# The last output tile of a feed-forward stage multiplied in two halves of 128 tokens

## What is computed

```python
def swiglu(x, wi, wo):
    a, b = jnp.split(x @ wi, 2, axis=-1)
    return (jax.nn.silu(a) * b) @ wo

# in second_block, for the one layer:
    h = h + 0.5 * rmsnorm(swiglu(rmsnorm(h, n[4]), ffn2_wi[l], ffn2_wo[l]), n[5])
return h[:, N_META:]
```

## Time and profile before

| | |
|---|---|
| Time, median of 3 runs | 1010.59 us (1009.25 to 1010.59) |
| Time of the profiled execution | 1010.97 us |
| Its span in the trace | 1009.1 us |
| PE busy | 989.7 us, 98% of the span |
| PEld busy | 973.7 us, 96% |
| POOL busy | 752.5 us, 75% |
| DVE busy | 549.5 us, 54% |
| ACT busy | 486.5 us, 48% |
| Granted TensorE clock, mean over the span | 0.99 |

### The profile page before, as it was taken

How to read it: one execution, slowest core, us unless ns; L and a number is a source line. 1 busy time by engine, 2 the same in 40 slices (tenths; PEclk the granted TensorE clock), 3 DMA queues, 4 the chain that set the end, 5 groups by cost and what they waited for, 6 DMA issues and landing times.

```text
span 1009.1 us, 21532 instructions
## 1 busy us (share of the span) xinstructions
PE 989.7 (98%) x8151; PEld 973.7 (96%) x8151; DVE 549.5 (54%) x931; ACT 486.5 (48%) x749; POOL 752.5 (75%) x588
## 2 busy tenths in 40 slices
PE   9999999999999999999999999999999999999996
PEld 7999999999999999999999899999999989999996
DVE  5945984547644444601874783476656574445103
ACT  6634324446654444444566643433264564444541
POOL 2896666666999888999389844667549539999993
PEclk9999999999999999999999998999999999999998
DMA  9564434343565555565454223443226736665661
GB/s 308 178 200 142 125 106 134 120 143 97 177 194 182 177 169 174 159 176 183 135 172 147 88 85 101 126 136 116 86 82 189 236 101 198 194 190 181 185 179 56
DMA packets 48345, 154.63 MB, mean 153 GB/s; under 512 B 6060, under 2 KB 11188, under 8 KB 48280
## 3 DMA queue, kind: packets, MB, share of 16 engines
q1 hardware_dynamic: 46128, 151.33, 48.6%
q10 hardware_dynamic: 2152, 2.38, 0.7%
HBM read 151.59 MB, written 2.10 MB: 152 GB/s over the span
## 4 chain that ended last, share of the span: by engine, by line
PE 87%; DVE 6%; ACT 3%; POOL 2%; DMA 1%; issue 1%; SPq 0%; DVEq 0%; ACTq 0%
PE panel L1721 70%; PE panel L1779 3%; PE aux L1880 3%; POOL wlo L644 1%; DMA memk<-in_mem_panels 1%; PE aux L2134 1%; PE aux L2145 1%; PE panel L1815 1%; PE aux L2107 1%; DVE h L1107 1%; DVE tmp L1101 1%; PE aux L2175 1%; PE aux L2184 1%; PE aux L1787 1%; DVE xl L1090 1%
## 5 line engine op out<-in xcount | busy, mean ns | idle before, releaser
L644 POOL TENSOR_TENSOR wlo<-raw,whi 128x512 fp32r<-128x512 f32 x548 | 727.7, 1357 | 234.7 <-ACT whi L739 211.6
L1721 PE MATMUL panel<-xh,whi 128*128 128x256 f32 (+2 forms) x1440 | 416.9, 290 | 3.5 <-DVE xl L1090 1.3
L1721 PE MATMUL panel<-xh,wlo 128*128 128x256 f32 (+2 forms) x1440 | 409.9, 285 | 0.0
L1721 PE MATMUL panel<-xl,whi 128*128 128x256 f32 (+2 forms) x1440 | 409.5, 284 | 0.0
L739 ACT ACTIVATE whi<-raw 128x1024 fp32r<-128x1024 f32 x280 | 293.9, 1053 | 200.6 <-PE panel L1721 167.4
L1721 PEld LDWEIGHTS panel<-xh,whi 128*128 128x128 f32 x1440 | 273.3, 190 | 5.6 <-issue 2.0
L1721 PEld LDWEIGHTS panel<-xh,wlo 128*128 128x128 f32 x1440 | 273.3, 190 | 0.0
L1721 PEld LDWEIGHTS panel<-xl,whi 128*128 128x128 f32 x1440 | 272.8, 189 | 0.1
L1721 PE MATMUL panel<-hh,wlo 128*128 128x272 f32 (+1 forms) x352 | 100.5, 286 | 0.0
L1721 PE MATMUL panel<-hh,whi 128*128 128x272 f32 (+1 forms) x352 | 100.2, 285 | 0.0
L1721 PE MATMUL panel<-hl,whi 128*128 128x272 f32 (+1 forms) x352 | 99.9, 284 | 0.0
(11 more groups left out here) (336 smaller groups left out, 1575.2 us busy)
## 6 DMA issues: line engine op xcount, KB each, us to landing
raw<-in_panels SPq DMA_DIRECT2D x232, 512.0 KB, 3.5
raw<-in_down SPq DMA_DIRECT2D x32, 448.0 KB, 3.3
raw<-in_down SPq DMA_DIRECT2D x16, 512.0 KB, 3.5
memk<-in_mem_panels SPq DMA_DIRECT2D x4, 512.0 KB, 7.9
memx<-in_mem SPq DMA_DIRECT2D x4, 256.0 KB, 5.5
h<-in_x SPq DMA_DIRECT2D x1, 1024.0 KB, 8.6
spill<-h ACTq DMA_DIRECT2D x1, 1024.0 KB, 4.6
h<-spill ACTq DMA_DIRECT2D x1, 1024.0 KB, 7.2
```

The costliest lines, as they stand in the source:

```text
L644: ins = nc.gpsimd.tensor_tensor(wlo[:, slot, half], raw[:, slot, half], whi[:, slot, half].bitcast(f32), ALU.subtract)
L1721: ins = M(bank[:, 0:w], wt[:, slot, P * t:P * t + P], x[:, kk, c0:c0 + w], start=first and m == 0 and n == 0, stop=last and m == len(pairs ...
```

## The change

- `down_loop(1, ...)` and `norm_stat(8)` on TensorE are replaced by `down_in_halves()`. It walks over the 24 panels without a hardware loop, with the wait for `lo_ready` of every panel. Tiles 0 to 6 are multiplied as before. For tile 7 it multiplies all 22 slices for tokens 0 to 127 into one bank, and then for tokens 128 to 255 into the bank after it (that of tile 4). Each is 66 matmuls of 128 columns.
- The norm sum is made for each half. That of half 0 is put between the products of half 1, before slice 7; that of half 1 follows at the end.
- ACT squares, and takes logarithm and exponential, half by half. DVE copies half by half (with a wait of the copy on itself), and then for each half weighs 2 x (4 tiles x 128 tokens) and adds 2 x (4 tiles x 128 tokens).
- The four stores are now 4 tiles x 128 tokens each.

The diff without the renamed parameters of the helpers and the new semaphores:

```diff
-QUARTERS = [(0, 1), (2, 3), (4, 5), (6, 7)]
+QUARTERS = [(half, part) for half in range(2) for part in range(2)]
...
-    uses += [("stat", n) for n in (6, 7, 8)]
+    uses += [("stat", n) for n in (6, 7, 8, 9)]
...
+        def last_bank(half):
+
+            return pb[(DOWN2_O + 7 + half) % 4]
...
-            for t, u in QUARTERS:
-
-                sp.wait_ge(h_ready, tile_done(8, u))
-                sp.dma_start(a["out"][:, t:u + 1, :], h[:, t:u + 1, META:LEN]).then_inc(stored, 16)
+            for m, (half, part) in enumerate(QUARTERS):
+
+                t, r = slice(4 * part, 4 * part + 4), slice(P * half, P * half + P)
+                sp.wait_ge(h_ready, 8 + WEIGHED[8] + m + 1)
+                sp.dma_start(a["out"][:, t, r], h[:, t, META + P * half:META + P * half + P]).then_inc(stored, 16)
             sp.wait_ge(stored, 16 * len(QUARTERS))
...
-            square_out(DOWN2_O, DOWN2_P, 3, 8)
-            post_root(8)
+            square_out(DOWN2_O, DOWN2_P, 3, 8, KT - 1)
+            ahead(PANELS - 1)
+            for half in range(2):
+                r = slice(P * half, P * half + P)
+                act.wait_ge(last_half, half + 1)
+                A(sq[:, KT - 1, r], last_bank(half)[:, 0:P], ACT.Square).then_inc(last_squared, 1)
+                bank, use = aux("stat", 8 + half)
+                aux_wait(act, use)
+                order(A(lnt[:, r], bank[:, 0:P], ACT.Ln, scale=1.0 / 1024.0, bias=eps))
+                A(rstd[:, r], lnt[:, r], ACT.Exp, scale=-0.5).then_inc(rstd_ready, 1)
...
-            take_out(DOWN2_O, 8, 40, 0.5)
-            combine(8)
+            take_out(DOWN2_O, 8, 40, 0.5, tiles=KT - 1)
+            for half in range(2):
+                r = slice(P * half, P * half + P)
+                dve.wait_ge(last_squared, half + 1)
+                order(TS(tmp[:, KT - 1, r], last_bank(half)[:, 0:P], vcol("gains", 47), 0.5, ALU.mult, ALU.mult))
+                dve.wait_ge(rstd_ready, 9 + half)
+                for part in range(2):
+                    t = slice(4 * part, 4 * part + 4)
+                    TT(tmp[:, t, r], tmp[:, t, r], bc(rstd[:, r], 1, 4), ALU.mult).then_inc(weighed, 1)
+                for part in range(2):
+                    t, own = slice(4 * part, 4 * part + 4), slice(META + P * half, META + P * half + P)
+                    dve.wait_ge(weighed, WEIGHED[8] + 2 * half + part + 1)
+                    TT(h[:, t, own], tmp[:, t, r], h[:, t, own], ALU.add).then_inc(h_ready, 1)
...
+            def down_in_halves():
+
+                parts = [(0, 8), (8, 7), (15, 7)]
+                pe.wait_ge(hid_low, 2 * FT - 2)
+                for n in range(24):
+                    i, part = n // 3, n % 3
+                    o, (k0, size) = DOWN2_O + i, parts[part]
+                    pe.wait_ge(lo_ready, DOWN2_P + n + 1)
+                    if n == 2:
+                        pe.wait_ge(hid_low, 2 * FT)
+                    if i == KT - 1:
+                        continue
+                    if part == 0:
+                        pe.wait_ge(bank_free[o % 4], o // 4)
+                    products(pb[o % 4], n % RING, [(t, k0 + t) for t in range(size)], hh, hl, 0, ROWS,
+                             part == 0, part == 2).then_inc(passed, 1)
+
+                def last_stat(half):
+
+                    stat, use = aux("stat", 8 + half)
+                    aux_open(use)
+                    r = slice(P * half, P * half + P)
+                    if half == 0:
+                        pe.wait_ge(summed, 6)
+                    M(stat[:, 0:P], ones[:], sq[:, 0, r], start=True, stop=False)
+                    pe.wait_ge(last_squared, half + 1)
+                    M(stat[:, 0:P], ones[:], sq[:, KT - 1, r], start=False, stop=True).then_inc(aux_full, 1)
+
+                for half in range(2):
+                    o = DOWN2_O + KT - 1 + half
+                    pe.wait_ge(bank_free[o % 4], o // 4)
+                    for part, (k0, size) in enumerate(parts):
+                        ins = products(last_bank(half), (21 + part) % RING, [(t, k0 + t) for t in range(size)], hh, hl, P * half, P,
+                                       part == 0, part == 2, lambda kk: last_stat(0) if half and kk == 7 else None)
+                    ins.then_inc(last_half, 1)
+                last_stat(1)
...
-            down_loop(1, DOWN2_O, DOWN2_P, ROWS)
-            norm_stat(8)
+            down_in_halves()
```

More of the change, by code:

```diff
@@ L509, in build @@
         mg_low = sem("mg_low")
+        last_half = sem("last_half")
+        last_squared = sem("last_squared")
         raw_ready = [sem(f"raw_ready{i}") for i in range(RING)]
@@ L561, in build @@
         LATE = {4: 0, 6: 1, 8: 2}
-        TILES = {4: PAIRS, 6: PAIRS, 8: QUARTERS}
+        TILES = {4: PAIRS, 6: PAIRS}
         WEIGHED = {4: 0, 6: len(PAIRS), 8: 2 * len(PAIRS)}
@@ L791, in combined, with square_out @@
                 return lambda kk: act.wait_ge(h_ready, tile_done(n, kk))
-            def square_out(first_o, first_p, each, n):
-                for i in range(KT):
+            def square_out(first_o, first_p, each, n, tiles=KT):
+                for i in range(tiles):
                     ahead(first_p + each * i + each - 1)
@@ L1150, in low_panel, with take_out @@
                 TT(wlo[:, p % RING, :], raw[:, p % RING, :], whi[:, p % RING, :].bitcast(f32), ALU.subtract).then_inc(lo_ready, 1)
-            def take_out(first_o, n, at0, factor, low_behind={}):
+            def take_out(first_o, n, at0, factor, low_behind={}, tiles=KT):
                 w = W[n]
-                for i in range(KT):
+                for i in range(tiles):
                     o = first_o + i
```

## The result

The changed kernel takes 1025.55 us, the median of 20 executions (1011.64 to 1032.92), against 1009.48 for the kernel before (20 executions, 1004.73 to 1011.1).

A forecast was written before the change was run, and what follows sets the result against it. TensorE, busy 98% of the span, was taken as the bound, with 10.2 us exposed behind its last product. 1.9 + 7.0 + 0.4 - 2.7 = +6.6 at full clock; with half clock +19.2 on 1010.6, so 1030 us, range 1016 to 1034.

The forecast's parts named there:

- The sum at full clock: Whole change if TensorE's clock held: added stall, products and norm sum less the tail's saving, +6.6 us.
- the fall: TensorE clock halves about 1 us after the halves start, without recovery; products at 0.21 us, +19.2 in all; chance 0.62.
- The stall: TensorE idle before the halves, waiting for GpSimd's last low part (panel 24): 1.9 us added.
- Products: Last tile's 132 products of 128 columns, paced by weight loads at 0.112 us each: 14.8 against 7.8, 7.0 more.
- The inserted norm sum: First half's norm sum between the second half's products on TensorE: 0.4 us more at full clock, its other work hidden.
- The tail: Stretch from last product to end, 10.2 us before: 2.7 saved, 2.4 of it from four VectorE pieces instead of eight.
- The stores: Four final stores with 512-byte runs and twice the packets: 0.2 us longer, between 0 and 0.75.
- The loop written out: TensorE's body, a loop of two turns before, written out: nothing taken for it.
- the third rival: Streaming, not the weight load, paces the narrow products at 0.06 us: -0.3, 1010.3 us, not slower; chance 0.05.
- the mixer's falls: Two clock falls after TensorE idles earlier in the program, near 577 and 601 to 611, used as evidence; one short fall 1.7 us.
- the first (the clock holds: +6.6, 1016 to 1020): TensorE's clock holds or falls only briefly during the halves: +6.6, 1017.2 us, or 1019 with a short fall; chance 0.24.
- The second (two records to a product): Narrow products go like plain fp32, two records of 0.11 us each: +21.4 in all, 1032 us; chance 0.06.

The follow-up runs named there:

- experiment 5: Changed kernel with GpSimd making the last weight panel's low part twice, so TensorE idles longer before the halves: 1033.85, 1034.06, 1034.4 and 1034.5 us, ratio 1.0239.
- experiment 7: Changed kernel without the stall, the last tile's narrow products loading 64 weight columns instead of 128 (upper 64 features left out): 1005.96 us, ratio 0.9965.
- experiment 6: Changed kernel with the last tile kept as 66 wide products and the old order of waits, only the close going by halves: 1008.96 us, ratio 0.9978.
- experiments 5 to 8: Second group of four kernels: longer stall, close alone by halves, half the weight columns, halves streaming all 256 columns; the kernel before beside them had median 1010.59 or 1010.54.
- first group of runs: Four kernels: stall removed (1015.34 us), stall filled with matmuls (1013.65), stall alone before wide products (1009.48), stall and narrow products with the old close (1018.05).
- experiments 3 and 8: The second of this pair: changed kernel, stall kept, each half's 66 products streaming all 256 columns: 1016.08 us, ratio 1.0065.
- experiment 3: Kernel before with its loop written out and the last tile waiting for panel 24 at once, products and close unchanged: 1009.48 us, ratio 1.0007.

## Why the prediction was right and wrong

The median, 1025.55, lies in the range and 4.5 us under the forecast. The sum at full clock was right to 0.1 us, and the fall, forecast at 12.6 us, costs some 13.8. **What failed is the step that took the fall as certain**: "So I expect the fall, about 1 us after the start, and no recovery". "No recovery" held where the long fall came, in the trace of experiment 5 and, by times and mean clocks, in the upper group. That it would come did not hold: 12 of 20 executions have the long fall and 8 don't, and the forecast had one outcome at 0.62 and the other at 0.24 as if the kernel would be the one or the other. It is both, by execution. The mean of all 20 is 1022.7, 13.8 us above the kernel before and not 19; 6.6 and the fall's 13.9 in 12 of 20 executions would give 14.9.

Step by step, forecast and measured:

- **The stall**: 1.9; 1.93 measured, with the releaser that was named.
- **Products**: 0.112 each, 14.8 for all; 0.111 to 0.112, and 9.90 + 4.99 = 14.9. The reason held too (experiment 7). The Trainium skill, "TensorE: Matmul & The Clock Gate", section "Back-to-back issue gap", has about 81 ns at 128 columns; the trace doesn't agree, and the estimate of +2.5 us from it would have been 4 us short.
- **The inserted norm sum**: 0.4; 0.27 + 0.22 = 0.5. The rest of the first half's close was hidden, as forecast: its last addition ended at 1005.2, 1.5 us ahead of the last product's end, and its stores were issued at 1004.62 and 1005.22.
- **The tail**: 2.7 saved, to 7.5; the last product ends at 1006.66 and the span at 1014.0, 7.35, where it was 10.2, so 2.9 saved. VectorE 2.4 as worked out. The norm sum's matmul pair takes 0.50 where the one piece of the earlier trace rows took 0.71, 0.2 as forecast.
- **The stores**: 0.2 assumed, between 0 and 0.75. From the last addition to the end it is 3.0 in both kernels, so 0 on the path.
- **The loop written out**: nothing; experiment 6 has it too and is no slower than the kernel before.
- **The sum**: 6.6; 24.6 - 18.05 = 6.6.
- **The clock**: a full fall was priced at 19.2 - 6.6 = 12.6 us. Between the medians of the two groups lie 12.3, between their means 13.8, between the traces of experiment 5 and of the changed kernel 13.9. A product at half clock was taken at 0.21; it takes 0.213. In experiment 5 products and inserted norm sum take 28.95 us (995.62 to 1024.57) where the forecast had 27.6: the fall comes 0.3 us after the start, not 1.0, which puts 6 more products at 0.213 (0.6 us), 0.213 instead of 0.21 is 0.4 over the rest, and the inserted norm sum takes 0.96 where 0.8 was taken.
- **The chances**: the third rival, the one case not slower, has 0.05, but "same" and "faster" together only 0.04; the two don't agree by 0.01.

The 4.5 us between forecast and median are then these. The median falls into the lower end of the twelve, because eight executions lie below it; the twelve's own median is 1027.1, 1.6 higher. The forecast was added to 1010.6 for the kernel before, from three runs; over 20 it is 1009.5, 1.1 less. The other 1.8 I put on the mixer's falls, which the clocks show less often in these twelve: eight are at 0.980 or higher, which is some 41 us at half clock or less and leaves no room for the mixer's fall of 10 us beside the long one of 36; only four, at 0.976 or lower, have it. Of the 29 executions of the kernel before beside experiments 5 to 8 nineteen are at 0.992 or lower, 16 us and more at half clock; some 5.4 of these are the idle end of its span (1003.7 to 1009.1 is at 0.50), the rest needs the fall of 10. Why they should be rarer no run tells, and 20 executions may be luck. The means depend less on where a middle falls: the twelve lie 19.3 above the kernel before, where 19.2 was forecast. That is so close partly by luck, since the fall costs 1.2 more than its price and rarer falls in the mixer take about as much off.

The spread within each group is those falls, by the list of clocks. A span of 1009.8 at 0.999 has 2 x 0.001 x 1009.8 = 2 us at half clock, no more than the idle end of the profiled span, and one of 1015.5 at 0.992 has 16. In the upper group 1023.3 us (the execution of 1025.16) at 0.982 gives 37 us, just the length of experiment 5's fall (995.94 to 1032.1 is 36.2), and 1029.4 to 1030.2 us at 0.976 give 49, which is that and the two falls of the mixer, 3.4 and 10.2 (experiment 5's profile has all three, and 0.976). So all 20 times need only one kind of event at the end, present or not, on top of the spread that the kernel before has too. This is worked out from mean clocks, and wouldn't show a fall of 3.4 us behind the stall for certain; of an upper execution of the changed kernel there is no trace.

What the experiments settle of the fall, in executions that stand in an upper group:

```
idle before    products after      fell and stayed
none           narrow              0 of 11 (no stall)   0 of 8 (stall filled)
1.7 to 1.9     256 columns wide    0 of 12 (one wide tile)  0 of 12 (two wide halves)
1.7 to 1.9     narrow              12 of 20 (changed)   2 of 7 (old close)
4.85           narrow              4 of 4
```

In these runs both are needed, as the forecast had it. The idle sets it off, and the narrow stream keeps it down: behind wide products the clock fell for 3.4 us in both profiles and recovered. Within the first group of runs alone, for the idle ahead of narrow products, it is 2 of 7 against 0 of 19, which is thin; the case rests on the changed kernel's 12 of 20 and experiment 5's four beside it. What decides in which executions 1.9 us of idle are enough is open. The Trainium skill, "TensorE: Matmul & The Clock Gate", section "Why this matters for your kernels", warns only of idle gaps longer than these, so by it the clock holds in every execution. The traces of experiments 3 and 8 don't agree: falls after 1.72 and 1.93 us.

Of the rivals, the first (the clock holds: +6.6, 1016 to 1020) is what 8 of 20 executions did, at +5.3 by the medians and +5.5 by the means; the profiles put the change itself at 6.6. The second (two records to a product) is out: one record each at 0.112. The third (the stream sets the pace) is out in the changed kernel, and experiment 7, where the load is halved, gives what it promised: -2.3 in the end stage, where the rival's -0.3 without the stall of 1.9 is -2.2.

Could a version beat the kernel before? Without the stall the split costs 4.5 us. The close alone by halves gives 0.4 us in the trace, and 12 executions can't tell it from nothing. Splitting only the last of the three panels, which would add a third of the extra products, wasn't tried.

## What to carry to other kernels

Before you split a matmul's moving side to let the work behind it start earlier, look at what sets the spacing: if it is the weight load (here 0.111 us a product when 128 columns stream, 0.119 when 256 do), each half costs nearly as much as the whole, and the price is nearly the whole tile again (7.1 us for a tile of 7.8). When you write a loop of waits out by hand, see which wait comes to stand ahead of which work; here a wait that had belonged to the last third of a tile moved ahead of all of it. And count a short idle stretch by what follows it: ahead of wide products it cost up to 1.8 us more than itself here, ahead of a narrow stream it could halve the clock to the end, in some executions only, so that a few runs or one profile can miss it.

## What the runs showed that I had not expected

- The same program, on the same data, has the full fall in 12 of 20 executions. One profile (1.00 throughout) and the median (1025.55) tell different stories, and both are true.
- A fall that comes and goes within 3.4 us is hard to see in the times of this kernel: experiment 3's profile has 3.4 us more in its end stage, and its 12 executions a ratio of 1.0007 [0.9986, 1.0028], with times spread over 7 us. A profile tells of its own execution only.
- At half clock the loads slow down as well: a load's record is 0.33 us (0.19 at full clock), and the spacing of 128-column products goes from 0.112 to 0.213 (experiment 5). That of 256-column products goes from 0.119 to 0.213 (experiment 3), so the load-bound stream loses at least as much.
- Stores in runs of 512 bytes take 35.8% of 10 us on the DMA engines, 3.6 us, against 3.0 us for runs of 1024 (33.2% of 9 us), with twice the packets: a fifth more engine time, and none of it shows on the path: 3.0 us from the last addition to the end in both.
